# The second feed-forward's down projection as seven half-sized products, on one Trainium2 core

## The reference

```python
hn = rms_norm_2(h, norm2_g[i])
ff = jnp.square(jax.nn.relu(jnp.einsum('bsd,df->bsf', hn, w_ff1[i])))   # 512 x 4096
h = h + jnp.einsum('bsf,fd->bsd', ff, w_ff2[i])                          # 4096 x 1024
hg = rms_norm_2(h, norm3_g[i])
```

## Time and profile before

| | |
|---|---|
| runs | 2021.79, 2021.79, 2022.31 us (median 2021.79) |
| profiled execution | span 2020.1 us from first to last instruction; its own whole time is not listed apart, the runs are 1.7 us above the span |
| TensorE busy | 1995.6 us, 99% of the span |
| VectorE, ScalarE, GpSimd busy | 1136.5, 816.5, 109.8 us |
| chain that ended last | TensorE 96%, VectorE 2%, ScalarE 1% |
| mean granted TensorE clock | 0.998 of full speed |

### The profile page before, as it was taken

One profiled execution on the slowest core, in us unless ns is written; L12 is line 12 of the kernel. 1 busy time (PEld: TensorE's weight loads), 2 busy tenths in 40 slices (PEclk: granted clock), 3 DMA queues, 4 the chain that ended last, 5 costly groups with the idle time before them and its releaser, 6 DMA issues.

```text
span 2020.1 us, 23761 instructions
## 1 busy us (share of the span) xinstructions
PE 1995.6 (99%) x9734; PEld 1647.2 (82%) x9734; DVE 1136.5 (56%) x1618; ACT 816.5 (40%) x1162; POOL 109.8 (5%) x120
## 2 busy tenths in 40 slices
PE   7999999999999999999999999999999999999998
PEld 7887788878888888888888687888888888888886
DVE  6847647576544675366368978743435444234346
ACT  5647633456323333133342635532333433123145
POOL 0004300221000000000010400000000000000000
PEclk9999999999999999999999999999999999999999
DMA  4320023211423333232333132232322233233232
GB/s 135 105 83 22 22 84 102 86 63 63 146 94 94 84 104 101 87 105 85 103 126 105 42 95 89 79 102 86 105 98 90 85 103 104 84 115 98 91 106 82
DMA packets 164441, 184.45 MB, mean 91 GB/s; under 512 B 6759, under 2 KB 125798, under 8 KB 164334
## 3 DMA queue, kind: packets, MB, share of 16 engines
q1 hardware_dynamic: 161006, 175.03, 27.1%
q10 hardware_dynamic: 2624, 5.78, 0.8%
q0 software_dynamic: 704, 2.13, 0.3%
HBM read 180.81 MB, written 2.12 MB: 91 GB/s over the span
## 4 chain that ended last, share of the span: by engine, by line
PE 96%; DVE 2%; ACT 1%; issue 0%; DMA 0%; POOL 0%; SPq 0%; DVEq 0%; ACTq 0%; POOLq 0%
PE ps L453 29%; PE ps L455 29%; PE ps L454 29%; PE ps L580 2%; PE ps L615 1%; PE ps L596 1%; PE ps L652 1%; PE ps L841 1%; ACT HH L1390 0%; DMA W<-in_w_in_dram 0%; DVE arena L2697 0%; PE ps L829 0%; DVE HL L2025 0%; DVE WL L1908 0%; PE ps L763 0%
## 5 line engine op out<-in xcount | busy, mean ns | idle before, releaser
L1908 DVE TENSOR_TENSOR WL<-W,WH 128x2048 fp32r<-128x2048 f32 (+2 forms) x162 | 367.6, 2271 | 356.3 <-ACT WH L1340 355.9
L453 PE MATMUL ps<-HH,WH 128*128 128x512 f32 (+1 forms) x1464 | 559.1, 382 | 3.5 <-DVE HL L2025 3.5
L455 PE MATMUL ps<-HH,WL 128*128 128x512 f32 (+1 forms) x1464 | 556.3, 380 | 0.0
L454 PE MATMUL ps<-HL,WH 128*128 128x512 f32 (+1 forms) x1464 | 556.1, 380 | 0.0
L1340 ACT ACTIVATE WH<-W 128x2048 fp32r<-128x2048 f32 (+2 forms) x163 | 307.3, 1887 | 278.1 <-DMA W<-in_w_ff_dram 115.4
L453 PEld LDWEIGHTS ps<-HH,WH 128*128 128x128 f32 x1464 | 275.3, 188 | 57.6 <-DVE HL L2025 2.6
L455 PEld LDWEIGHTS ps<-HH,WL 128*128 128x128 f32 x1464 | 275.3, 188 | 52.3
L454 PEld LDWEIGHTS ps<-HL,WH 128*128 128x128 f32 x1464 | 275.4, 188 | 51.7 <-issue 0.2
L453 PE MATMUL ps<-WH,arena_r 128*128 128x512 f32 (+1 forms) x616 | 239.2, 388 | 0.0
L455 PE MATMUL ps<-WH,arena_r 128*128 128x512 f32 (+1 forms) x616 | 239.0, 388 | 0.0
L454 PE MATMUL ps<-WL,arena_r 128*128 128x512 f32 (+1 forms) x616 | 239.0, 388 | 0.0
(11 more groups left out here) (376 smaller groups left out, 2275.9 us busy)
## 6 DMA issues: line engine op xcount, KB each, us to landing
W<-in_w_in_dram SPq DMA_DIRECT2D x50, 1024.0 KB, 5.1
W<-in_w_ff_dram SPq DMA_DIRECT2D x32, 1024.0 KB, 5.2
W<-in_ffn_w_up_dram SPq DMA_DIRECT2D x44, 512.0 KB, 4.8
W<-in_w_gate_dram SPq DMA_DIRECT2D x16, 1024.0 KB, 4.9
W<-in_ffn_w_down_dram SPq DMA_DIRECT2D x10, 1024.0 KB, 5.0
W<-in_w_out_dram SPq DMA_DIRECT2D x8, 1024.0 KB, 5.0
W<-in_w_branch_dram SPq DMA_DIRECT2D x8, 1024.0 KB, 5.0
W<-in_w_br_ssm_dram SPq DMA_DIRECT2D x4, 1024.0 KB, 4.9
```

What stands on the lines that cost most here:

```text
L453: pe.matmul(out_, st[0], mv[0], start=first, stop=False)
L454: pe.matmul(out_, st[0], mv[1], start=False, stop=False)
L455: return pe.matmul(out_, st[1], mv[0], start=False, stop=last)
L1908: dve.tensor_tensor(WL[:, j % RING, 0:n], W[:, j % RING, 0:n], plain(WH[:, j % RING, 0:n]), ALU.subtract).then_inc(slab_lo, 1)
```

## The change

The stages `ff2a`, `down2a`, `ff2b`, `down2b` become one stage, `ffn2`, of four chunks. A chunk takes four slabs of `w_ff1` (eight feature tiles, in four pairs) and multiplies them by 8 x 128 rows of `w_ff2`. The down product of a chunk is seen as a 2 x 2 block product: tokens in two halves of 256, features by even and odd tile, output columns in two halves of 512. In the form of Strassen and Winograd it takes seven products of blocks, here called parts P1, P5, P2, P6, P3, P7, P4 in the order in which they run, in place of eight. A part is one slab of 48/2 = 24 matmuls: two token tiles, four pairs, three matmuls.

The seven parts need sums of blocks on both sides. On the feature side VectorE makes S1 to S4 of each pair (256 columns each) beside the blocks A11, A12, A22, and seven "forms" per pair are split into high and low parts: form a (A11), forms b (A12, A22, S1) and forms c (S2, S3, S4). On the weight side GpSimd makes T1 to T4 from the raw blocks B11, B12, B21, B22 of a chunk, four subtractions or additions of 128 x 2048: T3 = B22 - B12, T2 = T3 + B11, T1 = B12 - B11 in place, T4 = B21 - T2. The raw blocks and the `w_ff1` slabs of a chunk lie in seven places (three of `W`, four in the arena). GpSimd writes T3, T2 and T4 into places that `w_ff1` slabs of the same chunk held before, and low parts still overwrite the raw weights they belong to, so VectorE waits in `sums_of` until every sum that reads a block is made. The results of parts are added up in PSUM without a reset: banks 0 and 1 hold P1, then P1+P6, then +P7, then +P4; banks 4 and 5 hold P5 and P5+P3; banks 2 and 3 hold P2; VectorE adds each stage to the place of X it belongs to (`add_part`), and TensorE goes on accumulating in a bank when that read is done (`chain_read`). Only banks 6 and 7 are left for the feature tiles.

```diff
+        def chunk_slots(c):
+            w = [(f2_slabs[0] + j) % RING for j in range(RING)]
+            if c == 0:
+                return dict(s=(w[0], w[1], w[2], w[0]), b11=3, b12=4, b22=5, b21=6, t3=w[1], t2=w[2], t4=w[0])
+            o = chunk_slots(c - 1)
+            n = dict(s=(o["b11"], o["b12"], o["b21"], o["b11"]), b11=o["b22"], b12=o["t3"], b22=o["t4"], b21=o["t2"],
+                     t3=o["b12"], t2=o["b21"], t4=o["b11"])
+            if c == CHUNKS - 1:
+                n.update(s=(*n["s"][:3], n["s"][1]), t3=n["s"][0], t2=n["s"][2], t4=n["s"][1])
+            return n
...
+            def part_products(c):
+                for m, (name, f, group, source, t0, cols) in enumerate(PARTS):
...
+                    w = slab(PAIRS, 512)
+                    for t in range(2):
...
+                            pe.wait_ge(chain_read, 8 * c + {"P6": 0, "P3": 2, "P7": 4, "P4": 6}[name] + t + 1)
...
+                        for k in range(PAIRS):
+                            if t == 0:
+                                forms = a_forms if f == 0 else b_forms if f <= 3 else c_forms
+                                pe.wait_ge(forms, PAIRS * c + k + 1)
...
+            def chunk_weights(c):
...
+                sp.wait_ge(*release[f2_slabs[11 * c + (1 if c == CHUNKS - 1 else 0)]])
+                first_weights(c, 3)
...
+                def sum2(c):
+                    s = chunk_slots(c)
+                    pool.wait_ge(b11_in, 16 * (c + 1))
+                    pool.wait_ge(*slab_before(c, "t2"))
+                    pool.wait_ge(t3_made, c + 1)
+                    pool.tensor_tensor(raw_slot(s["t2"])[0], raw_slot(s["t3"])[0], raw_slot(s["b11"])[0], ALU.add)\
+                        .then_inc(t2_made, 1)
...
+                for c in range(CHUNKS):
+                    sum3(c)
+                    sum2(c)
+                    sum1(c)
+                    sum4(c)
...
+            def act_ffn2():
...
+                def second_tile(i, n, last):
+                    relu(i, 1)
+                    split(n + 1 if last else n + 2)
+                    act.wait_ge(s1_made, i + 1)
+                    high(i, 1, 3)
...
+                    act.wait_ge(s4_made, i + 1)
+                    high(i, 4, 3)
...
+                        relu(i, 0)
+                        act.wait_ge(squared, 2 * i + 1)
+                        high(i, 0, 1)
...
+            def sums_of(c, source):
+                if source == "b11":
+                    dve.wait_ge(t2_made, c + 1)
+                    dve.wait_ge(t1_made, c + 1)
...
+            def dve_ffn2():
...
+                for c in range(CHUNKS):
+                    for j in range(4):
+                        i, n = 4 * c + j, f2_slabs[11 * c + j]
+                        if j > 0:
+                            second_tile(i - 1)
+                            split(n + 2)
+                            low(i - 1, 1, 3, b_forms)
+                            low(i - 1, 4, 3, c_forms)
+                        else:
+                            split(n + 2)
+                        first_tile(i)
+                    n = f2_slabs[11 * c + 4]
+                    second_tile(4 * c + 3)
+                    low(4 * c + 3, 1, 3, b_forms)
+                    split(n + 2)
+                    low(4 * c + 3, 4, 3, c_forms)
+                    for m in range(7):
+                        if m > 0:
+                            split(n + m + 2)
+                        for t in range(2):
+                            if c < CHUNKS - 1 or m < 5:
+                                add_part(c, m, t)
```

More of the change, by code:

```diff
@@ L295, in param, with win, xn_at @@
             col[name] = start
+        def win(c0, c1, name="w_in"):
+            return A[name][0, :, c0:c1].rearrange("(k p) n -> p k n", p=P)
+        def xn_at(n, t):
+            off = XN + t * DM if n not in XN_OF else XN_OF[n][t // 2] + t % 2 * DM
+            return at(off, DM)
         def turned(s):
@@ L403, in loaded @@
         def loaded(i):
-            return sum(len(slabs[j][2]) for j in range(i % RING, i + 1, RING))
+            return sum(len(slabs[j][2]) for j in range(i % RING, i + 1, RING) if j not in raw_of)
         def scan_slab(i):
@@ L444, in slab, with product @@
                 pe.wait_ge(slab_lo, i + 1)
-                return [w[:, i % RING, 0:kt * cols].rearrange("p (k n) -> p k n", k=kt) for w in (WH, WL)]
+                low = WL[:, i % RING, :] if i not in raw_of else raw_slot(raw_of[i])[1]
+                return [w[:, 0:kt * cols].rearrange("p (k n) -> p k n", k=kt) for w in (WH[:, i % RING, :], low)]
             def slab_read():
                 release[-1] = (pe_done, len(DONE))
[L450 to L455, removed]
+            def product(out_, st, mv, first, last, chained=False):
+                pe.matmul(out_, st[0], mv[0], start=first, stop=False, skip_group_check=chained)
+                pe.matmul(out_, st[0], mv[1], start=False, stop=False, skip_group_check=chained)
+                return pe.matmul(out_, st[1], mv[0], start=False, stop=last, skip_group_check=chained)
             def gemm_f(name, w, kt, c0, tiles, src, n0=0, between=None):
@@ L1092, in column_sums, with pe_ffn2 @@
                 pe.matmul(b[:, :], ones[:, :], src, start=True, stop=True).then_inc(pe_done, 1)
[L1094 to L1101, removed]
+            def pe_ffn2():
+                for c in range(CHUNKS):
+                    for j in range(4):
+                        i, n = 4 * c + j, len(slabs)
+                        f2_slabs.append(n)
+                        if c > 0:
+                            raw_of[n] = chunk_slots(c)["s"][j]
+                        w = slab(KT, 256, win(i * 256, i * 256 + 256, "w_ff1_2"))
+                        if i == 0:
+                            gemm_f_by_halves(("f1", i), w, 2)
+                            ring[:] = [6, 7]
+                        else:
+                            gemm_f(("f1", i), w, KT, 0, 2, hn)
+                        slab_read()
+                    part_products(c)
+                ring[:] = list(range(NB))
@@ L1384, in act_norm, with added @@
             def act_norm(n, gain, tag=None):
+                def added(t):
+                    if tag == "ffn2":
+                        taken(act, ("dn2", CHUNKS - 1, "C" if t < 2 else "A", t % 2))
+                    else:
+                        taken(act, (tag, t, 1))
                 def evict(half):
@@ L1413, in act_norm @@
                         evict(0)
-                    taken(act, (tag, t, 1))
+                    added(t)
                     square(t, n)
-                split(slab_of[tag, 0, 1] + 2)
+                if tag != "ffn2":
+                    split(slab_of[tag, 0, 1] + 2)
                 evict(1)
@@ L2053, in dve_norm @@
                     dve.wait_ge(x_again, 16)
[L2054 to L2059 removed]
+                if tag == "ffn2":
+                    add_part = dve_ffn2()
+                    for m in (5, 6):
+                        for t in range(2):
+                            add_part(CHUNKS - 1, m, t)
+                            if m == 5:
+                                made(t)
+                else:
+                    for t in range(NT):
+                        add(tag, t, 0)
+                    for t in range(NT):
+                        add(tag, t, 1)
+                        if 1 <= t < NT - 1:
+                            made(t - 1)
                 lows(0, 0, KT // 2)
```

272 lines of the change are left out of this document (217 added, 55 removed).

## The result

The changed kernel takes **2078.11 us** (median of 4 runs, 2076.64 to 2079.96), the kernel before, measured beside it, 2021.79 us (4 runs). The ratio is 1.0279, 95% interval 1.0264 to 1.0294: 2.8% slower. The profiled execution has a span of 2075.7 us against 2020.1, 55.6 more; the forecast had 46.8 more and 2068.6 us.

What follows compares the result with a forecast made beforehand. TensorE's queue sets the time (96% of the chain). Gain and costs, -21.8 + 32.6 + 6.0 + 4.8 + 1.6 + 11.0 + 12.55 = +46.8, give 2068.6 us; own range 2058 to 2079, wider range 2053 to 2085.

Steps and rivals of the forecast that it cites:

- 96 matmuls x 0.2265: Down product: 672 matmuls in place of 768, each worth its start-to-start distance on TensorE, 21.8 us less, the whole gain.
- waits on bank 7, four: Middle of each chunk: TensorE waits 8.15 us behind GpSimd's T2 and T1, 32.6 us over four chunks.
- clock falls, six: One fall to clock 0.50 behind each TensorE wait over 8 us, 1.5 us each.
- T3 makes bank 7 late: Chunks 1 and 2: T3 ahead of the second pair's first square makes bank 7 0.8 us late, 1.6 us in all.
- T4 against form a: Last pair: T4 can hold VectorE's square and form a at the shared port, 1.2 us per chunk, 4.8, bounds 0 and 16.4.
- last load, wait alone: Last chunk: bank 6 comes late behind the fourth w_ff1 slab's load and copy, 9.5 us without the clock fall.
- P4, wait alone: Last chunk: P4 waits 10.55 us because VectorE splits two gate slabs ahead of its reads of P7.
- the price of a sum: GpSimd's 128x2048 sum taken as 3.72 us, from 1.906 us for a two-input 128x1024 op; far bounds 1.82 and 7.2.
- Rival 2: GpSimd slower than the doubled row: 2096 us at 7.2 per sum, 2082 half way, 2075.6 at the skill's 4.6; 12%.
- Rival 3: Clock falls for longer, or after shorter waits too: 6 to 12 us more, about 2078 us; 15%.
- one of the forecast's three cases: P1's wait beside T4: 0.4 us if nothing is held, 4.1 if GpSimd precedes the square, 0 or 2.5 if the clock shifts.
- Rivals 1 and 4: First: port free, clock stays up, 2054.8 us, 17%. Fourth: sums done by third slab's end, 2025 or 2014 us, 4%.

Runs made afterwards that it cites:

- e7: Changed kernel with VectorE making the sums in another order, last chunk's fourth slab split later, P7/P4 adds before gate slabs, ScalarE high parts before slab copies: 2000.94 us.
- e8: Changed kernel with GpSimd's T2 and T1 taking a second operand that repeats over 64 columns, result not the reference's: 2071.95 us.
- e5: Changed kernel with VectorE making the four sums at the place in its list where it waited for GpSimd's: 2054.97 us.
- e6: Changed kernel with VectorE making the sums in another order and the low part of B11 ahead of no eviction: 2024.94 us.
- e3: Changed kernel, sums still on GpSimd, with VectorE taking the low parts of P1's and P5's weights later, behind forms: 2079.15 us.
- e1: Changed kernel with the reads of P7 and P4 put ahead of the gate slab splits they stood behind: 2066.31 us.
- e2: Changed kernel with the last chunk's fourth w_ff1 slab split one pair later, loaded as before: 2068.01 us.
- e4: Changed kernel with each GpSimd sum issued as two of 128x1024 in place of one of 128x2048: 2075.66 us.

## Why the prediction was right, and where its sizes were off

| term | forecast | measured |
|---|---|---|
| 96 matmuls x 0.2265 | -21.8 | -21.8 |
| waits on bank 7, four | 32.6 | 38.0 (9.5 each) |
| clock falls, six | 9.0 (6.0, and 1.5 in each of the last two terms) | 14.0 |
| T3 makes bank 7 late | 1.6 | 2.4 |
| T4 against form a | 4.8 | 1.4, at form b |
| last load, wait alone | 9.5 | 9.6 |
| P4, wait alone | 10.55 | 9.9 |
| transposes; load of `p` | 0.5; none | 0.3; 0.8 |
| sum | +46.8 | +54.6 (span: +55.6) |

The first line is the number of matmuls times their distance in both columns; e7, with nearly all waits gone, is 22.3 us below the kernel before.

The direction and all the long waits came as written, at the places and with the releasers named. The step that gave most of the remaining 8.8 us is **the price of a sum**. The forecast went by the nearest row of the trace, 1.906 us for 1024 columns, and took 3.72 for twice its size. Its own sign, sums of 3.6 to 3.9 us, did not come: e8 has 3.69 with a second operand that repeats; with two full operands it is 4.5 to 4.6. The size of the wait follows from it with one line through three kernels: 4.91 us at 2.21 per sum (e5), 7.79 at 3.65 (e8), 9.51 at 4.55 (after), start to start, all twice the sum plus 0.45 within 0.05; the forecast's form, twice the sum plus 0.7, was nearly that. Rival 2, as worded for the skill's figure, named this cause: 4.6 per sum, 2075.6 us. Rival 3's about 2078 is nearer to the 2078.11, but by luck: it kept sums of 3.72 and put all of the difference on the clock, which has 5.0 of it. The Trainium skill, "GPSIMD Engine Reference", section 3.1, lists 4.497 us for a two-input float32 add of 2048 columns on GpSimd and 2.293 us on VectorE; the traces have 4.51 and 2.29. Of the 8.8 us the sums' size is 5.4 (38.0 less 32.6) and 0.8 at T3.

**The clock** was the second: 1.5 us a fall from the earlier trace rows, measured 2.0 to 2.6. It makes 5.0 us, just under the 6 to 12 of rival 3. That row had other matmuls (384 columns) and weak work before, no full stop; which of these matters is open, and a fall of 1.5 comes here too (e6, before P4). e5 adds that a wait of half the length costs nearly as much (1.7 to 2.6).

**The shared port** worked as told but hit elsewhere. Form a was done before T4 began in every chunk, as one of the forecast's three cases had it, and the square of the last pair's second tile then took 4.6 to 4.9 us where it takes 0.69, which held up the last b forms that P5 needs, 0.3 to 0.6 us each (chunk 1):

```profile
1752.85 0.42 DVE L2992 TENSOR_TENSOR arena_r<-arena,arena_r 128x256 fp32r<-128x256 f32 x1
1754.37 4.91 DVE L2985 TENSOR_TENSOR arena<-arena 128x512 f32<-128x512 f32 x1 [1.09 <-ACT arena L2031]
```

So this term was too large by 3.4. e3 shows what else it can do: where VectorE has work during three sums, its list loses nearly their full length, of which, by the estimate there, about 4 us reach TensorE in a chunk.

**The two waits of the last chunk** were right within 0.1 and 0.7 us; e1 and e2 each took one away; e1 gave back the wait and its fall, e2 10.1 of 12.1 us. The load of `p` behind the norm (0.8 us) was not looked for. Rivals 1 and 4 are out: the port costs, the clock falls, and T2 and T1 are ready 9.1 us behind the slab. About 1 us of the span is not accounted for by these terms.

That the form of the product does not cost the time is shown: with the same products and the same sums, made by VectorE at other places, and with the last chunk's lists put right, the kernel is the fastest of all (e7). The loss lies in which engine makes the sums, in what order, and in what stands behind them.

## What to carry to other kernels

Before moving work to an idle engine, look for who waits for it in a tight list. Here GpSimd's sums also held two-input work on VectorE for up to their whole length, and VectorE, 79% to 81% busy from 1600 to 1900 us with them (e7), made the same sums in half the time without a wait of TensorE. Before doubling the nearest row, compare its operands with those of the new instruction, not only its size. Behind a long wait, add the clock fall, and look in each in-order list, of every engine, for what stands behind the one instruction that waits (a slab split ahead of a bank's read cost 12 us here, and moving it brought them back).

## What the runs showed of the hardware that was not expected

- A two-input GpSimd operation of 128x2048 takes 4.5 to 4.6 us with both operands read in full and 3.69 with a second operand that repeats over 64 columns; as two halves it takes 4.65 to 4.73 where VectorE leaves it alone.
- Short VectorE operations (0.42 us) that start during such a sum take 4.6 to 4.8 us each, one per sum: in e3's rows the two engines take turns by instruction. Two halves let VectorE in earlier (a square of 2.88 us in e4 in place of 5.10).
- The granted clock falls to 0.50 behind a wait of 4.91 us as behind one of 9.5, and each fall costs 1.5 to 2.9 us of matmul time over all runs. Behind the waits of 1.1 and 1.3 us it stayed at 1.00.
